# Two transformer blocks on one core: 64 bytes between high and low weights, and stage-wise places for activations and products

## The reference

```
h = norm(a * h + 0.5 * swiglu(h, gate1, up1, down1))    # 1024 -> 2816 -> 1024
h = norm(a * h + mixer(h @ w_in) @ w_out)
h = norm(a * h + 0.5 * swiglu(h, gate2, up2, down2))
swiglu(x, g, u, d) = (silu(x @ g) * (x @ u)) @ d
```

## Time and profile before

| | us |
|---|---|
| time, median of 3 (1993.54 to 1994.13) | 1993.56 |
| profiled execution: time | 1994.2 |
| profiled execution: span in the trace | 1992.4 |
| TensorE busy | 1976.9 (99%) |
| VectorE busy | 1429.0 (72%) |
| ScalarE busy | 1019.4 (51%) |
| GpSimd busy | 152.7 (8%) |

### The profile page before, as it was taken

One profiled execution on the slowest core, in us unless ns is written; L12 is line 12 of the kernel. 1 busy time (PEld: TensorE's weight loads), 2 busy tenths in 40 slices (PEclk: granted clock), 3 DMA queues, 4 the chain that ended last, 5 costly groups with the idle time before them and its releaser, 6 DMA issues.

```text
span 1992.4 us, 42293 instructions
## 1 busy us (share of the span) xinstructions
PE 1976.9 (99%) x16150; PEld 1936.5 (97%) x16150; DVE 1429.0 (72%) x2593; ACT 1019.4 (51%) x1525; POOL 152.7 (8%) x192
## 2 busy tenths in 40 slices
PE   9999999999999999999999999999999999999998
PEld 9999989999999999899999999999999999999998
DVE  6774887886688769888868775667756775667763
ACT  4433686554455447765446444564444443555443
POOL 0001122000100011210010000010000000100000
PEclk9999999999999999999999999999999999999999
DMA  7454423545454544245554664335454555435554
GB/s 258 172 203 165 170 86 128 190 168 196 157 182 175 188 150 164 86 174 193 184 188 152 223 220 179 128 146 192 179 215 165 190 201 193 148 125 180 189 208 150
DMA packets 46830, 346.66 MB, mean 174 GB/s; under 512 B 5344, under 2 KB 6416, under 8 KB 9232
## 3 DMA queue, kind: packets, MB, share of 16 engines
q1 hardware_dynamic: 44416, 335.63, 46.5%
q0 software_dynamic: 2320, 9.74, 1.5%
HBM read 344.29 MB, written 1.07 MB: 173 GB/s over the span
## 4 chain that ended last, share of the span: by engine, by line
PE 88%; DVE 6%; ACT 2%; DVEq 1%; issue 1%; DMA 0%; ACTq 0%; POOL 0%; SPq 0%
PE ps L589 28%; PE ps L591 28%; PE ps L590 28%; DVE w_lo L1909 2%; ACT w_hi L1235 1%; DVE cst L2378 0%; DVE pj L2357 0%; PE ps L1135 0%; DVE pj L2354 0%; ACT scratch L1586 0%; PE ps L1100 0%; DVE scratch L2323 0%; DMA raw<-in_w_up 0%; PE ps L925 0%; PE ps L936 0%
## 5 line engine op out<-in xcount | busy, mean ns | idle before, releaser
L1909 DVE TENSOR_TENSOR w_lo<-raw,w_hi 128x1024 fp32r<-128x1024 f32 (+1 forms) x582 | 748.7, 1313 | 167.4 <-ACT w_hi L1235 165.4
L1235 ACT ACTIVATE w_hi<-raw 128x1024 fp32r<-128x1024 f32 (+1 forms) x582 | 634.9, 1121 | 140.4 <-PE ps L591 126.5
L589 PE MATMUL ps<-x_hi,w_lo 128*128 128x256 f32 (+3 forms) x2416 | 693.0, 287 | 2.7 <-DVE x_lo L1996 1.4
L591 PE MATMUL ps<-x_hi,w_hi 128*128 128x256 f32 (+3 forms) x2416 | 685.5, 284 | 0.0
L590 PE MATMUL ps<-x_lo,w_hi 128*128 128x256 f32 (+3 forms) x2416 | 680.6, 282 | 0.0
L589 PEld LDWEIGHTS ps<-x_hi,w_lo 128*128 128x128 f32 x2416 | 454.6, 188 | 11.1 <-issue 5.9
L590 PEld LDWEIGHTS ps<-x_lo,w_hi 128*128 128x128 f32 x2416 | 455.4, 188 | 0.8
L591 PEld LDWEIGHTS ps<-x_hi,w_hi 128*128 128x128 f32 x2416 | 454.4, 188 | 0.0
L589 PE MATMUL ps<-hid_hi,w_lo 128*128 128x256 f32 (+1 forms) x1536 | 435.5, 284 | 0.7 <-DVE hid_lo L2107 0.4
L590 PE MATMUL ps<-hid_lo,w_hi 128*128 128x256 f32 (+1 forms) x1536 | 434.0, 283 | 0.0
L591 PE MATMUL ps<-hid_hi,w_hi 128*128 128x256 f32 (+1 forms) x1536 | 433.4, 282 | 0.0
(11 more groups left out here) (330 smaller groups left out, 1538.9 us busy)
## 6 DMA issues: line engine op xcount, KB each, us to landing
raw<-in_w_up SPq DMA_DIRECT2D x176, 1024.0 KB, 4.8
raw<-in_w_down SPq DMA_DIRECT2D x64, 1408.0 KB, 6.0
raw<-in_w_in SPq DMA_DIRECT2D x36, 1024.0 KB, 4.8
raw<-in_w_out SPq DMA_DIRECT2D x16, 1024.0 KB, 4.9
cst<-row_copy POOLq DMA_DIRECT2D x2, 1088.0 KB, 8.6
raw<-in_w_up SPq DMA_DIRECT2D x4, 512.0 KB, 6.8
cst<-in_consts POOLq DMA_DIRECT2D x1, 1537.5 KB, 6.5
prm<-in_prm POOLq DMA_DIRECT2D x2, 690.0 KB, 7.5
```

What stands on the lines that cost most here:

```text
L589: mm(dst, w_lo[:, j, cols], xa, start=first, stop=False)
L591: return mm(dst, w_hi[:, j, cols], xa, start=False, stop=last)
L1235: fn(w_hi[:, j, c], raw[:, j, c], ACT.Copy).then_inc(hi_done, 1)
L1909: v.tensor_tensor(w_lo[:, j, c], raw[:, j, c], w_hi[:, j, c].bitcast(F32), ALU.subtract)\
```

## The change

A buffer of 16 floats (64 bytes) is put between w_hi and w_lo, and the one ahead of x grows from 16 to 64 floats, so that w_lo begins 64 bytes later and all that follows 256 bytes later. In block 2 a variable `stage`, set while each engine's program is written out, picks where x and hid begin in their buffers (in floats, high and low apart) and the pitch of their chunks: six entries for x (first feed-forward part, mixer, second feed-forward part, of two layers), four for hid. Block 1 has stage -1, which keeps offsets and pitches. No instruction is added or removed. The buffers and what is computed stay the same.

```diff
--- before.py
+++ after.py
@@ -205,8 +205,9 @@
 
         raw = sb("raw", [P, 2, 2 * W_WIDE])
         w_hi = sb("w_hi", [P, 2, 2 * W_WIDE], F32R)
+        sb("gap", [P, 16])
         w_lo = sb("w_lo", [P, 2, 2 * W_WIDE], F32R)
-        sb("gap0", [P, 16])
+        sb("gap0", [P, 64])
         x_hi_all = sb("x_hi", [P, KD * X_PITCH], F32R)
         sb("gap1", [P, 96])
         x_lo_all = sb("x_lo", [P, KD * X_PITCH], F32R)
@@ -234,6 +235,8 @@
         HID_BYTES = NF * T1 * 4
         hid_at = nc.sbuf_base - 2 * HID_BYTES
         SCRATCH = 2 * NF * T1
+        X_LAYOUT = ((0, 0, T1), (32, 0, T2), (0, 0, T2), (32, 32, T2), (48, 16, T2), (48, 48, T2))
+        HID_LAYOUT = ((0, 0, T1), (16, 16, T2), (48, 16, T2), (16, 32, T2))
         scr = nc.alloc_sbuf_tensor_at("scratch", [P, SCRATCH], F32, offset=hid_at)
         ps = ctx.enter_context(nc.psum_tensor("ps", [P, 8, 512], F32))
 
@@ -260,19 +263,24 @@
             return buffer[:, 0:n * pitch].rearrange("p (k t) -> p k t", k=n)
 
         x_hi, x_lo = chunks(x_hi_all, KD, X_PITCH), chunks(x_lo_all, KD, X_PITCH)
-        xt_hi, xt_lo = chunks(x_hi_all, KD, T2), chunks(x_lo_all, KD, T2)
+        stage = [-1]
         hid_hi, hid_lo = chunks(hid_hi_all, NF, T1), chunks(hid_lo_all, NF, T1)
-        hidt_hi, hidt_lo = chunks(hid_hi_all, NF, T2), chunks(hid_lo_all, NF, T2)
 
         plain_hi, plain_lo = (chunks(plain[:, i * PLAIN_HALF:i * PLAIN_HALF + KD * X_PITCH], KD, X_PITCH) for i in range(2))
         squares = [pj[:, 0, :], pj[:, 1, :], std[:, 1, :], silu[:, 0, :], silu[:, 1, :], prod[:, 0, :], prod[:, 1, :],
                    std[:, 0, :]]
 
         def x_of(T):
-            return (xt_hi, xt_lo) if T == T2 else (x_hi, x_lo)
+            if T != T2:
+                return x_hi, x_lo
+            at_hi, at_lo, pitch = X_LAYOUT[stage[0]]
+            return chunks(x_hi_all[:, at_hi:], KD, pitch), chunks(x_lo_all[:, at_lo:], KD, pitch)
 
         def hid_of(T):
-            return (hidt_hi, hidt_lo) if T == T2 else (hid_hi, hid_lo)
+            if T != T2:
+                return hid_hi, hid_lo
+            at_hi, at_lo, pitch = HID_LAYOUT[stage[0] // 3 * 2 + (1 if stage[0] % 3 else 0)] if stage[0] >= 0 else (0, 0, T2)
+            return chunks(hid_hi_all[:, at_hi:], NF, pitch), chunks(hid_lo_all[:, at_lo:], NF, pitch)
 
         row_copy = nc.dram_tensor("row_copy", (SSD_HEADS // 2, 2, T1), F32, kind="Internal").ap()
         CONST_PAIR, CONST_STEP = 4, 1
@@ -1193,6 +1201,7 @@
             pe.wait_ge(ones_set, 1)
             for n in range(CLOCK_STEPS):
                 mm(ps[:, 7, 0:T2], rstd[:, 0:P], rstd[:, 0:T2], start=True, stop=True)
+            stage[0] = -1
             for l in range(DEPTH):
                 t0, q, r0 = l * TURNS1, l * 2, l * 3
                 T = OUT_T[l]
@@ -1210,6 +1219,7 @@
             for l in range(DEPTH):
                 t0, q, e0, r0 = l * TURNS2 + BLOCK2_TURN, l * 2 + 2 * DEPTH, l * 4 + EVENT2, l * 3 + 3 * DEPTH
 
+                stage[0] = 3 * l
                 if l == 0:
                     crossing_up(q, t0 + SEC2["ffn1"], e0, 3 * DEPTH - 1, T2)
                 else:
@@ -1217,7 +1227,9 @@
                 down(q, t0 + SEC2["ffn1"] + UP_T, r0, T2)
                 pe.wait_ge(prm_in, l * 16 + (16 * DEPTH + 16))
                 pe.wait_ge(consts_in, 16 * (1 + len(CONST_PARTS)))
+                stage[0] = 3 * l + 1
                 pieces = mixer2(l, t0 + SEC2["in"], e0 + 1, l * 3 + 1)
+                stage[0] = 3 * l + 2
                 out_proj(t0 + SEC2["out"], e0 + 2, r0 + 1, T2, (cat_hi2, cat_lo2), OUT2_BANK, pieces, CAT_ORDER)
                 up(q + 1, t0 + SEC2["ffn2"], e0 + 3, T2, {1: lambda: rms_mean_square(l * 3 + 2)})
                 down(q + 1, t0 + SEC2["ffn2"] + UP_T, r0 + 2, T2)
@@ -1874,17 +1887,21 @@
             for l in range(DEPTH):
                 t0, q, r0 = l * TURNS2 + BLOCK2_TURN, l * 2 + 2 * DEPTH, l * 3 + 3 * DEPTH
                 n0, s0 = l * 3 + NORM2, l * 3 + 1
+                stage[0] = 3 * l
                 up(q, t0 + SEC2["ffn1"], T2, crossing=l == 0)
                 act.wait_ge(prm_in, l * 16 + (16 * DEPTH + 16))
+                stage[0] = 3 * l + 1
                 down(t0 + SEC2["ffn1"] + UP_T, r0, True, s0, T2, "mixg")
                 second_pair(t0 + SEC2["in"], 1)
                 root(n0, T2, "eps2")
                 mixer2(l, t0 + SEC2["in"])
+                stage[0] = 3 * l + 2
                 out_proj(t0 + SEC2["out"], r0 + 1, True, s0 + 1, T2, "ffn2g")
                 second_pair(t0 + SEC2["ffn2"], 1)
                 root(n0 + 1, T2, "eps2")
                 up(q + 1, t0 + SEC2["ffn2"], T2)
                 if l < DEPTH - 1:
+                    stage[0] = 3 * l + 3
                     down(t0 + SEC2["ffn2"] + UP_T, r0 + 2, True, s0 + 2, T2, "nextg")
                     second_pair(t0 + TURNS2, 1)
                 else:
```

## The result

| | us |
|---|---|
| before, median of 7 (1992.82 to 1995.31) | 1993.89 |
| changed, median of 7 (1994.27 to 2001.32) | 1999.94 |
| ratio, changed to before | 1.0026, 95% interval 1.0016 to 1.0035 |
| profiled execution of the changed kernel: time, span | 1997.23, 1995.4 |

The change made the kernel slower by 0.26% by the ratio, 6.05 us by the medians, where 5.8 us less had been forecast. Two things are to be explained: the sign, and that executions of the changed kernel lie 7 us apart, those of the kernel before 2.5 us. (Of 53 more executions of the kernel before, in later comparisons, one took 1998.80 us and the others 1992.77 to 1995.32; what that one spent it on isn't recorded.)

The account below looks back on a forecast made before the run. TensorE was taken as the bound: number of matmuls times the interval between starts. The terms -2.1 - 4.3 + 0.6 = -5.8 us took 1993.6 to 1987.8 us, with a range of 1977 to 1997.

Parts of the forecast that it names:

- The other engines' cover: Other engines' work stays hidden behind TensorE; with accesses 10% dearer VectorE would still have 20 us left in its stage.
- I take this remainder as what the change sets: Distance from activations to weights modulo 256 is what the change sets; that hardware cares about 256 was assumed.
- the ranking of places: hid's remainders 0, 128 held faster than x's 64, 192; a full step between them taken as 1.1 ns per matmul.
- (a): 64 bytes between w_hi and w_lo: block 1's x and plain, 5664 matmuls at 0.37 ns, 2.1 us less.
- (b): x in the second block at new remainders: 3936 matmuls one step of 1.1 ns faster, 4.3 us less.
- (d): hid in the second block: layer 0's second part 0.6 us more; layer 1 taken as 0, bad end 1.2 more.
- my second support: Block 1's x with chunks 1152 bytes apart at 116.7 ns, cited for x in block 2 becoming faster.
- a third of a step: Block 1: only the last of three products streams while low weights load, so 0.37 ns of the 1.1 ns step.
- (c): x of layer 0's first feed-forward part, pitch 1088, 960 matmuls: taken as 0, bounds 0.8 us more and 1.1 less.
- The rival "slower": Low weights' new remainder costs block 1's x and plain 6.2 us, nothing won in block 2: 1999.8 us; chance 0.17.
- The rival "place doesn't matter": Interval may depend on how a stage is entered, no trend: 1993.6 us, up to 2 either side; chance 0.23.
- the rival of a larger gain: 116.7 ns is not the floor: two steps for block 2's x, a full step in block 1; 1979.4 us, chance 0.21.

Follow-up runs that it names:

- the shift by 256: Kernel before with 256 bytes more ahead of x and nothing else; 1994.32 against 1994.05 us, ratio 1.0001.
- the single distance: Both blocks left out, one product instead of three on TensorE, weights' start moved in 16-byte steps from 0 to 1008; 120.0 ns per matmul at 0.
- The map: Both blocks left out, TensorE alone runs the three products at 64 combinations of stream and low-weight remainders, two visits each; 113.3 to 122.2 ns per matmul.
- the first profile: Changed kernel, its profiled execution, nothing further altered; 1997.23 us, span 1995.4.
- the second: Changed kernel, same code profiled in another execution; 1998.61 us, span 1996.8.

## Why the prediction was wrong

- What bounds the kernel, and that only the interval can move the time: right. The other engines' cover held, the busy times of VectorE and ScalarE are the same to 0.6 us, and TensorE's busy time took up the whole difference. Its longest wait for another engine stayed at 1.4 us.
- "I take this remainder as what the change sets", modulo 256: right as far as the shift by 256 and the single distance show. That the place sets the interval: right, but it is the triple that does, and the entry draws among its values.
- The step that failed first is the ranking of places, on which (a), (b) and (d) rest. I read hid's 116.7 against x's 117.5 as a property of the pair 0, 128. The map has both at 117.8, and hid's 116.7 is the better of two draws; the earlier trace rows, the same place at 117.9, said so, and I put it into a rival instead of into the sum., my second support, was a draw too: 117.8 in the run shifted by 256. The places of block 2 before were at the common value or at a lucky draw, and of the places that block 2 moved to only (0, 128, 64) has shown a lower one.
- (a), a third of a step for the last of each three: the products don't add. At +64 the interval of 274 columns didn't move, that of 272 fell by 0.5 ns, of 258 rose by 1.1 in one execution and not in the other; -2.1 us was forecast; by the starts +0.1 came in the first profile and -1.7 in the second, where 272 columns ran at 124.5 and 258 at 120.0. That the second is near the forecast is luck: 1.6 of it is one stage, where I had spread 2.1 evenly over all of block 1's x and plain. I had also counted all of block 1's products among the turning places; the last ones have 256 columns and stand at (0, 128), which at +64 has three values, and they were 1.3 us longer in one profile, unchanged in the other.
- (b), -4.3 us: the one step down came in one stage of five (last x, -1.9), and in another execution the same stage was 4.4 us longer than that. Layer 1's first x rose by 1.3 ns (by the starts 118.8 in both profiles, the less frequent value of its triple), the mixers by 0.1 to 0.5. The sum had a slip too: layer 0's second part keeps its distances from the high weights, so by (a)'s own reasoning it was worth a third of a step, not the full step of 1.2 us that is in the 4.3. It stayed at 118.4.
- (c), taken as 0 with 0.8 us more as its bad end: 0.7 by the windows, 0.5 by the starts.
- (d): the direction of +0.6 was right and its size 0.7; for layer 1's products I took 0 with 1.2 as the bad end, they cost 1.7.
- The range, 1977 to 1997, left out 1999.94: its upper end kept 3.7 us of gain in block 2, where block 2 lost 1.8 in the first profile and 6.0 in the second by the starts.
- The rival "slower" named 1999.8, close to what was measured, but for block 1's x and plain; these came to +0.1 and -1.7 us in the two profiles. Its number was met by another mechanism. The rival "place doesn't matter" was wrong in its name and right that the change would draw the lot again; but the lot was drawn from the new places' values, which are mostly the same or worse, and not from the old ones'. What I had named as the sign for it, unequal intervals at equal places, came.
- "No row of 256 columns is below 116.6" stood against the rival of a larger gain. It was true of the trace, and no bound: 113.3 was three offsets away.

What stays open: why the place counts at all. The runs show the period, the size, differences already at 16 bytes, and that one stream with its weight loads suffices, but not what draws one value or another at a place, nor why (192, 192) and (64, 64) with low weights at 128 are the low ones.

## What to carry to other kernels

In a kernel that TensorE bounds, with a weight load for each matmul, the place of the streamed matrix against the weights can be worth something for nothing: up to 8% of the interval in the map of 256 columns in float32, 1.7% of the time in this kernel. Other types and widths were not measured. Measure it with TensorE alone over all places of the loop that the kernel runs, each entered several times, and take a place whose worst value is low, for that may be what the kernel gets; more visits can still show another value. A kernel whose times spread by several us with a steady clock may be standing on a place with several.

## What the runs showed of the hardware

- The interval of 256 columns with a load each ran from 113.3 to 122.2 ns at 2.4 GHz, by place, with all other engines idle. It repeats after 256 bytes as far as tried, and places 16 bytes apart differ: 120.0 at 0, 118.3 at 16, 116.7 at 208 with one stream and one set of weights.
- At some places it has two or three values, 115.6, 117.8 and 120.0 at (0, 128, 64), kept over a stage of 123 to 127 us and drawn anew by the next. Where a stage is interrupted it can change within it: 117.6 and then 113.3 ns at (192, 192, 0).
- By the Trainium skill, "TensorE: Matmul & The Clock Gate", Part 2, loading the next weights takes no read bandwidth from the running matmul, and "SBUF — State Buffer", section "SBUF: two separate sides", has TensorE wait for nobody. Neither page has the interval depend on addresses. The trace does: with nothing else running, the address of the weights alone moved it by 6.7 ns, from 113.3 to 120.0. Whether that is a wait or lost bandwidth, no run here shows.
